# Blocked scores in a gated recurrence, with a new ScalarE order, tiled norm sums and a new load order

## The reference

```python
xn = rmsnorm(h, norm_mix_g)
a, a_gate, q, f, i, g = split(xn @ w_in)        # six times 512 columns
y_conv = silu(groupnorm(causal_conv31(a * sigmoid(a_gate))))    # 8 groups of 64
y_hgrn = hgrn2(q, f, i, g)                      # 4 heads of 128
h = h + concat(y_conv, y_hgrn) @ w_out
h = h + peer(rmsnorm(h, norm_ffn_g))            # 16 of 16384 experts per head, 8 heads
out = rmsnorm(h, final_norm_g)

# hgrn2, per head: b = cumsum(log f); within a block of tokens
scores[t, s] = sum_k q[t, k] * k[s, k] * exp(b[t, k] - b[s, k])     # s <= t
out = scores @ v + (q * exp(b)) @ state
state = exp(b_last) * state + (k * exp(b_last - b)).T @ v
out = out * rsqrt(mean(out * out)) * norm_g * silu(g)
```

## Time and profile before

| | |
|---|---|
| median of three runs | 2818.68 us (2816.42 to 2819.83) |
| the profiled execution | 2820.35 us |
| its span, first to last instruction | 2818.5 us |
| mean granted clock of PE | 0.993 |
| PE busy | 2743.7 us, 97% |
| DVE busy | 2168.7 us, 77% |
| POOL busy | 1648.6 us, 58% |
| ACT busy | 1127.4 us, 40% |
| DMA | 657.91 MB, mean 233 GB/s |

### The profile page before, as it was taken

How to read it: one execution, slowest core, us unless ns; L and a number is a source line. 1 busy time by engine, 2 the same in 40 slices (tenths; PEclk the granted TensorE clock), 3 DMA queues, 4 the chain that set the end, 5 groups by cost and what they waited for, 6 DMA issues and landing times. The chain is left out here.

```text
span 2818.5 us, 46725 instructions
## 1 busy us (share of the span) xinstructions
PE 2743.7 (97%) x15776; PEld 1493.3 (53%) x15872; DVE 2168.7 (77%) x4223; ACT 1127.4 (40%) x1581; POOL 1648.6 (58%) x1504
## 2 busy tenths in 40 slices
PE   7999999999999999999999999899999999999998
PEld 3445744555666666656666665444444444444443
DVE  3999954223788999979999993777777777777778
ACT  4355743323444444446766763312211221221122
POOL 1332211111333444477767676788888888889884
PEclk9999999999999999999999999999999999999999
DMA  3231030111344555578888888899999999999995
GB/s 126 82 130 43 1 145 16 60 45 55 127 163 159 187 187 177 176 274 308 299 332 304 309 323 306 319 364 329 341 343 335 329 344 357 350 346 352 358 347 190
DMA packets 265233, 657.91 MB, mean 233 GB/s; under 512 B 17552, under 2 KB 116112, under 8 KB 261952
## 3 DMA queue, kind: packets, MB, share of 16 engines
q1 hardware_dynamic: 190992, 387.37, 38.5%
q0 software_dynamic: 74160, 269.52, 26.8%
HBM read 547.24 MB, written 110.10 MB: 233 GB/s over the span
## 5 line engine op out<-in xcount | busy, mean ns | idle before, releaser
L95 POOL TENSOR_TENSOR w_low<-w_ring,w_high 128x1024 f16<-128x1024 f32 x164 | 368.6, 2248 | 816.7 <-ACT w_ring L90 816.3
L1645 PE MATMUL psum<-region_y,w_high 128*128 128x384 f16 x2048 | 669.0, 327 | 12.3 <-POOL w_low L95 6.6
L1646 PE MATMUL psum<-region_y,w_high 128*128 128x384 f16 x2048 | 669.0, 327 | 0.0
L1647 PE MATMUL psum<-region_y,w_low 128*128 128x384 f16 x2048 | 669.0, 327 | 0.0
L2360 DVE TENSOR_TENSOR region_x<-region_x,psum 128x1024 f32<-128x1024 f32 x192 | 234.2, 1220 | 213.8 <-PE psum L2194 213.6
L2211 ACT ACTIVATE scores<-w_ring 128x1024 bf16<-128x1024 f32 x64 | 67.0, 1048 | 656.1 <-PE psum L2194 652.0
L1703 ACT ACTIVATE ge<-psum 128x384 f32<-128x384 f32 x256 | 124.9, 489 | 414.0 <-PE psum L1647 412.2
L2192 PE MATMUL psum<-scores,share 128*128 128x512 bf16 x737 | 280.6, 381 | 8.0 <-DVE region_x L2360 6.4
L2192 PE MATMUL psum<-scores,wh 128*128 128x512 bf16 x752 | 285.3, 379 | 2.3 <-POOL wl L2243 1.5
L2194 PE MATMUL psum<-scores,wl 128*128 128x512 bf16 x752 | 285.3, 379 | 0.8
L2193 PE MATMUL psum<-vl,wh 128*128 128x512 bf16 x752 | 285.2, 379 | 0.8
(11 more groups left out here) (316 smaller groups left out, 5497.8 us busy)
## 6 DMA issues: line engine op xcount, KB each, us to landing
w_ring<-in_u_t_dram SPq DMA_DIRECT2D x128, 512.0 KB
acts_dram<-ge SPq DMA_DIRECT2D x128, 384.0 KB, 2.8
gates_dram<-scores SPq DMA_DIRECT2D x24, 2048.0 KB, 9.2
scores<-gates_dram SPq DMA_DIRECT2D x30, 1536.0 KB, 16.3
scores<-acts_dram SPq DMA_DIRECT2D x30, 1536.0 KB, 19.6
w_ring<-in_v_t_dram SPq DMA_DIRECT2D x64, 512.0 KB, 10.6
more_v<-in_v_t_dram SPq DMA_DIRECT2D x64, 512.0 KB, 4.8
w_ring<-in_w_stream_dram SPq DMA_DIRECT2D x20, 512.0 KB, 3.5
```

Source lines behind the costliest of these rows:

```text
L95: pool.tensor_tensor(self.wl[:, s, :], self.wf[:, s, :], self.wh[:, s, :], ALU.subtract).then_inc(self.w_lo, 1)
L1645: pe.matmul(a, uh[:, par, row], xh[:, n, cols], start=(n == 0), stop=False)
L1646: pe.matmul(a, uh[:, par, row], xl[:, n, cols], start=False, stop=False)
L1647: last = pe.matmul(a, ul[:, par, row], xh[:, n, cols], start=False, stop=(n == KC - 1))
```

## The change

**Recurrence.** The scores of a level are computed only in the blocks that it needs. Each block is a matmul of its own, whose output stands at the partitions of its keys: one of 64x64 at level 0, two of 32x32 at level 1, four of 16x16 at level 2, and four tiles of 32x32 along the diagonal at the levels 3 to 6. Level 2 and the masked copies go to a compact `near_att` (32 columns a head), which ACT copies into the four diagonal tiles of `att`; PE waits for that before scores by values. The exponent of `near_q` is made by DVE, that of `k_end` inside ACT's activation with a bias, per head and first of all; POOL makes neither. ACT does `centered(n - 1)` in the middle of `levels(n)`.

**Norm sums.** Each sum of squares is four matmuls of 128 tokens, whose outputs stand at partitions 0, 32, 64 and 96 of one bank. Root and reciprocal are then 128 wide and 128 long, and each spread is four matmuls from 16 rows at these partitions. Both halves are float32; the three-part split is gone. ACT takes both roots before all eight silus, and DVE scales four units at a time.

**Load order.** In the middle stretch of select, SP issues the load of item `s + 3` at each second item ahead of the gates store.

**Combine.** Dots are accumulated in `dot` itself. DVE makes two low parts of group 1, after the fourth and the fifth add of group 0, and POOL tells the others of them after two gathers. `xtok` is loaded with the final gain once `acc_ok` is 2.

```diff
+    def blocks(l):
+        hs = CHUNK >> l
+        for first in range(0, P, 2 * hs if l < BY_BLOCKS else TILE):
+            if l < BY_BLOCKS:
+                t = slice(first + hs, first + 2 * hs)
+                yield slice(first, first + hs), t, t if l < 2 else slice(hs, 2 * hs)
+            else:
+                tile = slice(first, first + TILE)
+                yield tile, tile, slice(0, TILE)
@@ mixer, tensor
                     for hh in range(CG):
-                        last = pe.matmul(bank(SCORE[l % NS])[:, hh, :], keys[:, hh, :], queries[:, hh, :],
-                                         start=True, stop=True)
+                        for s, t, to in blocks(l):
+                            last = pe.matmul(bank(SCORE[l % NS])[s, hh, to], keys[:, hh, s], queries[:, hh, t],
+                                             start=True, stop=True)
...
                 gate_part(n, G_FIRST, G_SECOND)
+                pe.wait_ge(sc_ok, BASE + n * LC + LC)
@@ mixer, scalar
             def levels(n):
+                for hh in range(CG):
+                    last = act.activation(k_end[:, hh, :], b_blk[:, hh, :], ACT.Exp, scale=-1.0,
+                                          bias=b_blk[:, hh, P - 1:P])
+                last.then_inc(x_exp, 1)
                 for l in range(LEVELS):
...
+                    if n and l == CENTER_AT:
+                        centered(n - 1)
...
-                act.activation(k_end, k_end, ACT.Exp, scale=-1.0).then_inc(x_exp, 1)
...
                 act.activation(k_end_t, bank(2), ACT.Copy).then_inc(kt_ok, 1)
+                act.wait_ge(sc_ok, BASE + n * LC + LV)
+                for first in range(0, P, TILE):
+                    tile = slice(first, first + TILE)
+                    last = act.activation(att[tile, :, tile], near_att[tile, :, :], ACT.Copy)
+                last.then_inc(sc_ok, 1)
...
                 decays(n, n == 0)
-                centered(n)
+            centered(TB - 1)
@@ mixer, vector
-                for l in range(LEVELS):
+                for l in range(LV):
...
-                    dve.tensor_tensor(seg(lev[l], 2 * hs), bs, ref, ALU.subtract).then_inc(x_sub, 1)
+                    to = lev[l] if l < LEVELS else near_q
+                    dve.tensor_tensor(seg(to, 2 * hs), bs, ref, ALU.subtract).then_inc(x_sub, 1)
...
-                    mask = cm[:, (l - 1) * P:l * P].rearrange("p (a t) -> p a t", a=1).to_broadcast([P, CG, P])
-                    dve.copy_predicated(att, mask, bank(SCORE[l % NS])).then_inc(sc_ok, 1)
+                    mask = near_m[:, l - 1:l, :].to_broadcast([P, CG, TILE])
+                    dve.copy_predicated(near_att[:, :, :], mask, bank(SCORE[l % NS])[:, :, 0:TILE]).then_inc(sc_ok, 1)
@@ project_out, tensor
+            def stats(h):
+                for c in range(2 * CG):
+                    for q, tile in enumerate(TILES):
+                        last = pe.matmul(psum[tile, 6 + h, 0:P], stat[:, c * NSTAT:c * NSTAT + QUARTER],
+                                         squares(c, h)[:, q, :], start=(c == 0), stop=(c == 2 * CG - 1))
+                last.then_inc(stat_mm, 1)
+
+            def spreads(group):
+                h = UNITS[CG * group][1]
+                pe.wait_ge(rstd_ok, h + 1)
+                pe.wait_ge(scaled_ok, CG * group)
+                for i in range(CG * group, CG * (group + 1)):
+                    c = UNITS[i][0]
+                    for q, rows in enumerate(ROWS):
+                        last = pe.matmul(spread_out(i)[:, q, :], spread[rows, c, :], rstd[rows, h, :],
+                                         start=True, stop=True)
+                last.then_inc(spread_mm, 1)
@@ project_out, vector
+            invert(0)
             for h in range(NH):
+                if h == 1:
+                    residual(0)
+                scale(2 * h)
                 if h == 0:
+                    invert(1)
+                for i in range(PER_HALF * h, PER_HALF * h + CG):
+                    gate(i)
+                scale(2 * h + 1)
+                for i in range(PER_HALF * h + CG, PER_HALF * (h + 1)):
                     low(i)
@@ select_and_activate, sync
             def spread(s, par, n, j):
-                pick(s, par, n, j)
+                first = isinstance(n, int) and n == 0 and j == 0
+                pick(s, par, n, j, loaded=j % 2 == 0 and not first)
                 if j % 2 == 1:
 
+                    load(s + 3, 1 - par)
                     u = j // 2
                     sp.wait_ge(g_ok, 16 * n + (8 * u + 8))
@@ combine, gpsimd, group 1
                     for c in range(CPG):
-                        low_v(c)
+                        if c < POOL_LOW:
+                            low_v(c)
                         low_w(c)
                     indices()
-                    for i in range(len(CHUNKS_U)):
+                    for i in range(2):
+                        gather(i)
+                    pool.wait_ge(v_lo_dve, 2 * (CPG - POOL_LOW))
+                    pool.tensor_tensor(spare[:, TOLD + 1:TOLD + 2], zero[:, :], zero[:, :], ALU.add).then_inc(
+                        v_lo, CPG - POOL_LOW)
+                    for i in range(2, len(CHUNKS_U)):
                         gather(i)
@@ combine, vector
-                                             op1=ALU.mult, accum_out=dots[:, k:k + 1]).then_inc(row_used, 1)
-                    if k == U_ONE - 1:
-                        dve.wait_ge(row_used, used(g, True) + U_ONE)
-                        dve.tensor_copy(dot[:, 1, ds(U_ONE * g + U_DONE, U_ONE)], dots[:, :]).then_inc(dot_ok, 1)
+                                             op1=ALU.mult, accum_out=dot[:, 1, ds(U_ONE * g + (U_DONE + k), 1)]
+                                             ).then_inc(row_used, 1)
...
+                    if is_first(g) and EARLY_LOW <= q < EARLY_LOW + CPG - POOL_LOW:
+                        low_v(1, q - EARLY_LOW + POOL_LOW)
```

207 lines of the change are left out of this document (78 added, 129 removed).

## The result

The median is **2787.3 us** (2786.7 to 2788.3) against 2819.3 (2816.4 to 2821.4) for the kernel before, measured side by side: a ratio of 0.9892, 95% interval 0.988 to 0.9905. The forecast was 2789, range 2774 to 2812. So the total came out nearly as said. Of its four terms only C did, and most of what follows is about the other three.

The account below looks back on a forecast made before the run. TensorE, busy 97% of the span, was taken as the bound. Savings of 13 (recurrence) + 2 (norm sums) + 6.5 (load order) + 8 (combine) = 29.5 us from the median 2818.68 gave 2789 us, range 2774 to 2812.

Parts of the forecast that it names:

- A: Recurrence: centering copy moved and scores narrowed end the ScalarE-then-TensorE series; 13 us saved, bounds -26 and +17.
- the term of VectorE: Recurrence: VectorE needs 14.6 us a block plus some 0.4 of wait, 15.0, and sets the period of 15.1.
- B: Norm stage: sums and spreads split into 128-column matmuls in four tiles; 2 us saved, bounds -7 and +10.
- rival 5: Norm sums and spreads: all four tiles run at once, 7 to 8 us more saved, 2781 us; chance 0.12.
- 4 MB of w_out are there by 397, so they hide: Norm stage: w_out's loads, estimated from 353 GB/s, land by 397 and cost nothing.
- C: End of select: next load issued ahead of the gates store removes a TensorE stall; 6.5 us saved (2 to 9).
- rival 3: Select and combine: DMA takes back C, VectorE's new low parts half of D; 2800 us, chance 0.12.
- D: Start of combine: dots accumulated in place and two low parts moved to VectorE; 8 us saved (3 to 9).
- group 2, which has until 1866: Combine: gathers and value loads queued behind GpSimd's new wait are not due until 1866.
- Rival 1: Recurrence: 32-column records cost 0.056 us, TensorE binds at 20.0 a block; 2837 us, chance 0.06.
- Rival 2: Recurrence and norm sums: tiles don't overlap, period 15.5, A = 10, B = -7; 2801 us, chance 0.14.
- Rival 4: Recurrence: TensorE's clock falls to 1.2 GHz, about 70 us slower, 2880 us; chance 0.02.

Follow-up runs that it names:

- order_only: Kernel after with full-width scores and 512-column masked copies again, new ScalarE order kept; recurrence period 15.40 us.
- outputs_late: Kernel after with ScalarE's output and gate copies moved behind the block's score copies; ratio 0.9890 to the kernel before, recurrence 3.5 us shorter.
- same_tile: Kernel after with score and norm-sum matmuls issued tile by tile instead of alternating between tiles; 2790 us.
- halves: Kernel after with w_out's second half loaded first; first output matmul 12.5 us after the first norm sum, 4.7 less than in the kernel after.
- pool_peel: Kernel after with GpSimd's low parts of combine group 2 all ahead of that group's gathers; combine 3.3 us shorter.
- center_old: Kernel after with ScalarE's centering copy back behind the block's other work, narrow scores kept; recurrence period 17.07 us.
- dots_old: Kernel after with the five dots accumulated in their own tile and copied by VectorE again; combine 5.0 us longer.
- halves_fill: halves plus 22 identity matmuls in TensorE's pauses in the norm stage; ratio 0.9866 to the kernel before.

## Why the prediction came out as it did

**The bound read from the profile** held: what TensorE was given back early is there at the end, and from group 2 of the combine on the two traces run 33.6 us apart. (The terms and their forecast of 29.5 are of the profiled executions, which differ by 33.7; the medians differ by 32.0.)

**A (13, was 17.2): the mechanism held, and VectorE was rightly next; its price was wrong.** Order plus narrow scores break the series; order_only shows the 15.4 that TensorE's full-width work allows. The step that failed is the term of VectorE, 15.0 a block (14.6 and a wait). It measured 13.2. Its 15.44 of before contained operations that GpSimd held up:

```profile
306.82 1.04 POOL L822 TENSOR_TENSOR hg_rest<-region_k 128x512 f32<-128x512 f32 x1 [12.35 <-PE psum L589]
307.82 1.49 POOL L826 TENSOR_TENSOR glu<-region_k 128x512 f32<-128x512 f32 x1
```

The six subtractions in the earlier trace rows are 4.53 together, but step 0.60 each once GpSimd is silent: 0.93 of them was this, and 0.2 of the operation before them. Both went when GpSimd's two subtractions went, and the seventh costs 0.60, not the 0.755 taken from the swollen mean. A masked copy is 0.44, not 0.48. So 15.44 - 0.93 - 0.2 - 4x0.44 + 0.60 = 13.15, where the row gives 13.19. What stands between this and the period of 14.4 is 0.65 a block beside GpSimd's low parts (two in six blocks) and 0.53 of waits for ScalarE's score copies. outputs_late takes the second away, and VectorE then never waits. ScalarE is near: 12.4 of work, against 13.2 in the prediction.

**B (2, was 5.9): rival 5's mechanism, another limit.** All tiles at once is what same_tile shows, and the sums took 3.7 us where the rival had 3.6. By its sum B was 9 to 10. It was 5.9, since the step "4 MB of w_out are there by 397, so they hide", 13 us into the stage, failed: w_out was there after 17.2. halves gives what the chain alone allows, 12.5. And the slow clock, priced at 1.7 lost, was 13.7 us long, of which the part under output products, 383.6 to 388.5, cost half of 4.9, 2.5.

**C (6.5, was 7.4).** The step on the bus held in kind: later loads came late (1.4 and 1.7), which was rival 3 in part. Its size is not settled, as said.

**D (8, was 2.7): right up to group 1, then given back.** VectorE's adds (starts in us) date it:

```
add                      before      after     saved
first (group 0)         1812.75    1782.62     30.13
fourth                  1833.77    1794.45     39.32
twelfth (group 1)       1873.58    1835.89     37.69
fourteenth (group 2)    1884.02    1850.47     33.55
191st (last group)      2804.92    2771.27     33.65
```

7.6 us are won at the copy of the earlier trace rows, as forecast (8); at group 2 4.1 go again. The step that failed is "group 2, which has until 1866". The date was right: on the clock of before TensorE is due there at 1866.0 (1835.86 in after, which runs 30.1 ahead at the first add). But nothing was worked out for GpSimd, whose last low part of that group was ready just in time in the kernel before:

```profile
1870.94 1.65 POOL L2243 TENSOR_TENSOR share<-scores,share 128x768 bf16<-128x768 f32 x1
```

TensorE started the group at 1873.38, 0.8 us after the end of this row. In after TensorE would be there 37.5 us earlier, and the low part, in its old place among the gathers, ends at 1837.88, only 34.7 earlier. So TensorE stands 2.3 and then runs slow for 3.4. pool_peel removes the wait and the slow stretch.

**The other rivals.** Rival 1 (0.056 a record) fell: 0.010. Rival 2 (no overlap) fell by same_tile. Rival 3 (DMA) is in C; most of D was lost too, but to GpSimd's order and not to late rows, as pool_peel shows. Rival 4 (the clock) happened in small: 13.7 us at 1.2 GHz in the recurrence of after against 3.4 before, and center_old, with 30.7, shows that it can eat the gain of narrow work. What the rival leaned on was misread: before, the clock was 1.00 during the sums (384.0 to 395.3) and fell only behind them (0.77 from 395.3 to 408). The errors of A and B (4 too small each) were in part cancelled by that of D (5 too large). That 2789 was so near is luck.

## What to carry to other kernels

Before pricing the engine that binds next, clear its durations of what vanishes with the change: a mean that holds another engine's work is not a price. Then add back what still runs beside it. When a stall is removed, date every later deadline anew by the time won, and set against it when each helper engine, in its own order, is done: a slack of 0.8 us was enough before and not after. And give consecutive small matmuls to different tiles: the order of issue alone was worth a factor of 3 in the sums here.

## What the hardware showed

- Four 32-column tiles in turn ran at 0.027 us a record of 128 columns against 0.087 in one tile after another; 32-column records at 0.010 against 0.021.
- Operations of VectorE that read and write SBUF alone stood still while GpSimd worked, small ones too: a copy of 128x5 took 10.45 us in the earlier trace rows and 6.30 in dots_old, each until GpSimd's unbroken run of low parts ended, and in the recurrence of after the first subtraction of the row at 313.12 took 2.6 in place of 0.68, beside the low part at 312.96. The Trainium skill, "SBUF — State Buffer", section "SBUF: two separate sides", describes an exclusive lock held for the whole instruction; these rows agree, and add that a run of instructions can keep the other engine out from its first to its last.
- TensorE's granted clock fell to 1.2 GHz in the norm stage of halves for 10.2 us, with pauses and narrow products (0.73 over 19 us), and not at all in halves_fill, with 22 products of the identity in the pauses (1.00 over 18 us). That saved nothing in the stages, as the data were late anyway.
- In the recurrence of center_old it fell once in each of seven blocks, for 3.4 us behind a pause of about as long.
- Four loads of 64 KB took 7.0 us from GpSimd's queue beside 4 MB on SyncE's, and 2.6 ahead of them on SyncE's own.
